# One encoder step on one core: the rotation table in buffers of its own and split anew, two scan-matrix buffers, and loads and stores in another order

## The reference, cut to what matters

```python
h = rmsnorm(x) * (1 + scale) + shift            # scale, shift, gate = c @ w_ada + b_ada
q, k, v, iq, ik, iw, za, u, zs = split(h @ w_in)   # 5712 columns
# attention: an indexer scores keys, the top 256 are kept, softmax over them, then * silu(za)
# S5: per group of 16 channels a 64-dim complex diagonal state
lam_bar = exp(lam * dt); b_bar = (lam_bar - 1) / lam * b
h_t = lam_bar * h_(t-1) + b_bar @ u_t           # scan over positions, chunks of 64
y = re(c @ h_t) + d * u;  y = gelu(y) * sigmoid(gelu(y) @ w_glu + b_glu) * silu(zs)
out = x + gate * rmsnorm(concat(attn, y) @ w_out)
```

## Time and profile before

| what | value |
|---|---|
| median of 3 runs | 2255.09 us (2254.04 to 2257.56) |
| the profiled execution | 2255.6 us, its span in the trace 2253.8 us |
| mean granted clock of TensorE | 0.972 of 2.4 GHz |
| PE busy | 2107.7 us, 94% of the span |
| DVE busy | 1293.7 us, 57% |
| ACT busy | 717.1 us, 32% |
| POOL busy | 272.8 us, 12% |
| data moved | 292.90 MB, 130 GB/s on average |

### The profile page before, as it was taken

The page is one execution under the profiler, slowest core; times in us unless marked ns, Lnnn a source line. Parts: engine busy times, 40 slices in busy tenths (PEclk is TensorE's granted clock), DMA queues, the critical chain, the costliest instruction groups (busy, mean ns, idle before and its releaser), DMA issues. The chain is left out here.

```text
span 2253.8 us, 33057 instructions
## 1 busy us (share of the span) xinstructions
PE 2107.7 (94%) x12713; PEld 1860.7 (83%) x12713; DVE 1293.7 (57%) x2587; ACT 717.1 (32%) x1408; POOL 272.8 (12%) x560
## 2 busy tenths in 40 slices
PE   5898898999999999999999999599989899999996
PEld 4578797888899999999999999477877577777764
DVE  5555645344324788888877665466865354324445
ACT  5341122111124333233333221344544333223323
POOL 0254353355410000000000000000000100000000
PEclk9999999999999999999999999699999999999998
DMA  9973466665443333333333432663441232224666
GB/s 349 335 179 77 125 138 146 161 183 175 144 122 84 97 87 95 98 88 98 94 92 98 98 80 77 193 180 118 124 109 50 79 93 73 73 82 152 174 187 190
DMA packets 380718, 292.90 MB, mean 130 GB/s; under 512 B 125273, under 2 KB 317985, under 8 KB 379273
## 3 DMA queue, kind: packets, MB, share of 16 engines
q1 hardware_dynamic: 355906, 256.96, 41.6%
q10 hardware_dynamic: 23328, 30.03, 4.0%
q0 software_dynamic: 1328, 3.80, 0.5%
HBM read 230.51 MB, written 60.20 MB: 129 GB/s over the span
## 5 line engine op out<-in xcount | busy, mean ns | idle before, releaser
L1293 PE MATMUL ps_z<-h_hi,w_hi 128*128 128x384 f32 (+2 forms) x1936 | 666.4, 344 | 0.0
L1295 PE MATMUL ps_z<-h_hi,w_lo 128*128 128x384 f32 (+2 forms) x1936 | 657.0, 339 | 0.0
L1294 PE MATMUL ps_z<-h_lo,w_hi 128*128 128x384 f32 (+2 forms) x1936 | 656.8, 339 | 0.0
L1293 PEld LDWEIGHTS ps_z<-h_hi,w_hi 128*128 128x128 f32 (+1 forms) x1936 | 363.1, 188 | 15.6 <-issue 5.2
L1294 PEld LDWEIGHTS ps_z<-h_lo,w_hi 128*128 128x128 f32 (+1 forms) x1936 | 363.2, 188 | 5.1
L1295 PEld LDWEIGHTS ps_z<-h_hi,w_lo 128*128 128x128 f32 (+1 forms) x1936 | 362.8, 187 | 5.4
L877 DVE TENSOR_TENSOR w_lo<-w_raw,w_hi 128x512 fp32r<-128x512 f32 (+1 forms) x172 | 125.5, 730 | 352.8 <-ACT w_hi L543 351.1
L543 ACT ACTIVATE w_hi<-w_raw 128x512 fp32r<-128x512 f32 (+1 forms) x172 | 107.5, 627 | 262.9 <-DMA w_raw<-in_w_in 204.5
L1009 DVE MAX8 top<-score 128x8 f32<-128x1024 f32 (+5 forms) x192 | 171.1, 891 | 3.4
L1011 DVE MATCH_REPLACE8 score<-top,score 128x1024 f32<-128x1024 f32 (+5 forms) x192 | 168.2, 876 | 0.0
L2304 POOL DMA_DIRECT2D v_cached<-in_cache_v x8 | 6.0, 753 | 1157.1 <-POOLq L66 1133.2
(11 more groups left out here) (455 smaller groups left out, 3272.8 us busy)
## 6 DMA issues: line engine op xcount, KB each, us to landing
w_raw<-in_w_in SPq DMA_DIRECT2D x176, 256.0 KB, 3.1
wada<-in_w_ada SPq DMA_DIRECT2D x32, 1024.0 KB, 9.1
o_raw<-in_w_out SPq DMA_DIRECT2D x92, 256.0 KB, 3.1
wg<-in_w_ada SPq DMA_DIRECT2D x32, 512.0 KB, 5.0
zt<-z_sb ACTq DMA_DIRECT2D x28, 576.0 KB, 4.2
ssm_f<-in_w_out SPq DMA_DIRECT2D x52, 256.0 KB, 4.2
g_raw<-in_w_glu SPq DMA_DIRECT2D x24, 512.0 KB, 4.3
xs<-in_x_prompt SPq DMA_DIRECT2D x8, 1024.0 KB, 7.9
```

The source lines that it names most:

```text
L1293: M(to, w_hi[q][:, k, 0:m], h_hi[:, kk, cols], start=kk == 0, stop=False)
L1294: M(to, w_hi[q][:, k, 0:m], h_lo[:, kk, cols], start=False, stop=False)
L1295: return M(to, w_lo[q][:, k, 0:m], h_hi[:, kk, cols], start=False, stop=kk == KB - 1)
```

## The change

The change has these parts. A block `extra` of 8 KB a partition is set aside. GpSimd's two rotation buffers move there, so they overlap nothing; GpSimd makes six turns of the rotation table and VectorE two (slots 14 and 15), and GpSimd no longer waits for `c_mat_T`. The second `turn_c` moves from slot 12 to 13. Later a second `wmat` and `bslot` lie in `extra`, and batches alternate. The clearing of `taps` follows the first `pmat`. `load_states` moves from slot 36 to 35. The store of the last block has a semaphore of its own, `z_last`, which only the load of `za` in the next program awaits; that load becomes the last of the first four. `ROW_STEP` becomes 0, 2, 3, 5, 6 and so on, `gate_tanh(0)` and `gates(0)` move one step later. In `attend_samples` the two pieces of `w_out` are loaded after the keys of samples 2 and 3. In `project_out` the half-rows of pair 0 are stored from GpSimd's queue. Some semaphores are merged or divided, and the scratch for DMA descriptors is set to 8192.

```diff
--- before.py
+++ after.py
@@ -130,6 +130,8 @@
         w_hi = [sb(f"w_hi{q}", [P, QK, P], F32R) for q in range(4)]
+        extra = (nc.sbuf_base + 31) // 32 * 32
+        sb("extra", [P, 2048])
         z_sb = sb("z_sb", [P, TOK])
@@ -156,12 +158,15 @@
         turn_w = over(back + 35328, "turn_w", [P, 3, PAIRS, 8])
-        chunk = [[over(back + at, f"rot_chunk{i}_{at}", [P, 4, 2, 8, 16]) for at in ats] for i, ats in enumerate(((20992,), (12800, 16896)))]
-        chunk_w = [over(back + at, f"rot_work{i}", [P, 4, 8, 16]) for i, at in enumerate((25088, 27136))]
-        wmat, wtmp, pmat, ptmp, bslot, pout, taps, skip = placed(
-            keep["back_free"], ("wmat", [P, PAIR_BATCH, 2, STEP + 1, CH]), ("wtmp", [P, PAIR_BATCH, STEP + 1, CH]),
-            ("pmat", [P, PAIR_BATCH, 2, STEP, CH]), ("ptmp", [P, PAIR_BATCH, STEP, CH]), ("bslot", [P, 2, PAIR_BATCH, CH]),
+        chunk = [[over(back + at, f"rot_chunk{i}_{at}", [P, 4, 2, 8, 16]) for at in ats] for i, ats in enumerate(((extra - back, extra - back + 4096), (12800, 16896)))]
+        chunk_w = [over(back + at, f"rot_work{i}", [P, 4, 8, 16]) for i, at in enumerate((35328, 27136))]
+        wmat0, wtmp, pmat, ptmp, bslot0, pout, taps, skip = placed(
+            keep["back_free"], ("wmat0", [P, PAIR_BATCH, 2, STEP + 1, CH]), ("wtmp", [P, PAIR_BATCH, STEP + 1, CH]),
+            ("pmat", [P, PAIR_BATCH, 2, STEP, CH]), ("ptmp", [P, PAIR_BATCH, STEP, CH]), ("bslot0", [P, 2, PAIR_BATCH, CH]),
             ("pout", [P, PAIR_BATCH, 2, P]), ("taps", [CH, 2 * PAIR_BATCH, TAPS, CH]), ("skip", [CH, 2 * PAIR_BATCH, CH]))
+
+        wmat = [wmat0, over(extra, "wmat1", [P, PAIR_BATCH, 2, STEP + 1, CH])]
+        bslot = [bslot0, over(extra + 8 * PAIR_BATCH * (STEP + 1) * CH, "bslot1", [P, 2, PAIR_BATCH, CH])]
 
@@ -194,7 +199,7 @@
         rows_in, s5_in, bc_in, x_in, ada_in = sem("rows_in"), sem("s5_in"), sem("bc_in"), sems("x_in", 4), sems("ada_in", 7)
-        ident_step, ident_ok, c_copied, vec_T, vec_copied = (sem(n) for n in ("ident_step", "ident_ok", "c_copied", "vec_T", "vec_copied"))
+        ident_ok, c_copied, vec_T, vec_copied = (sem(n) for n in ("ident_ok", "c_copied", "vec_T", "vec_copied"))
         squared, var_ok, root_ok, x_scaled, norm_step = (sem(n) for n in ("squared", "var_ok", "root_ok", "x_scaled", "norm_step"))
@@ -209,7 +214,7 @@
         p_step, p_ok, p_T, p_copied, p_out = (sem(n) for n in ("p_step", "p_ok", "p_T", "p_copied", "p_out"))
-        bslot_ok, w_step, w_ok, q_stored = (sem(n) for n in ("bslot_ok", "w_step", "w_ok", "q_stored"))
+        bslot_ok, w_step, w_ok, q_stored = sem("bslot_ok"), sem("w_step"), sem("w_ok"), sems("q_stored", 2)
         k_mm, k_copied, skip_ok, taps_ok, taps_zero, toep_stored = (
...
@@ -251,6 +258,7 @@
         SCAN = BUILD + 2 * BATCHES + 2
+        POOL_TURNS, DVE_TURNS = 6, 2
         HALVES = PAIRS // 2
@@ -312,7 +320,7 @@
 
-            pairs = slice(12 * i + 4 * n, 12 * i + 4 * n + 4)
+            pairs = slice(4 * (POOL_TURNS * i + n), 4 * (POOL_TURNS * i + n + 1))
             mine = chunk[i][n % len(chunk[i])]
@@ -327,8 +335,8 @@
         def store_chunk(eng, i, n):
-            pairs = slice(12 * i + 4 * n, 12 * i + 4 * n + 4)
-            eng.dma_start(scr["rot"][:, pairs], chunk[i][n % len(chunk[i])][:].rearrange("p j r a b -> p j r (a b)")).then_inc(rot_out[i + n % len(chunk[i])], 16)
+            pairs = slice(4 * (POOL_TURNS * i + n), 4 * (POOL_TURNS * i + n + 1))
+            eng.dma_start(scr["rot"][:, pairs], chunk[i][n % len(chunk[i])][:].rearrange("p j r a b -> p j r (a b)")).then_inc(rot_out[2 if i else n % 2], 16)
 
@@ -393,7 +401,7 @@
                 sp.dma_start(scr["s5_out"][:, js],
-                             wmat[:, :, :, 1:].rearrange("p j r t c -> p j r (t c)")).then_inc(q_stored, 16)
+                             wmat[b % 2][:, :, :, 1:].rearrange("p j r t c -> p j r (t c)")).then_inc(q_stored[b % 2], 16)
 
@@ -496,22 +504,24 @@
                     store_inputs(batch_at(S - 2))
-                if 16 <= S < 21:
-                    sp.wait_ge(chunk_ok[1], S - 15)
-                    store_chunk(sp, 1, S - 16)
+                if 15 <= S < 15 + DVE_TURNS:
+                    sp.wait_ge(chunk_ok[1], S - 14)
+                    store_chunk(sp, 1, S - 15)
                 if G + 1 < N:
...
                     store_taps(batch_at(S - 3))
+                if S == SCAN - 3:
+                    load_states()
                 if S == SCAN - 2:
                     load_half(0)
-                    load_states()
                 if S == SCAN:
...
                     sp.wait_ge(toep_stored, 16 * STEP * BATCHES)
-                    sp.wait_ge(q_stored, 16 * BATCHES)
+                    for i in range(2):
+                        sp.wait_ge(q_stored[i], 8 * BATCHES)
                     sp.wait_ge(p_out, 16 * BATCHES)
@@ -569,7 +579,7 @@
                 else:
-                    act.dma_start(zt[col:col + m, c0:], z_sb[0:m, c0:]).then_inc(z_out, 16)
+                    act.dma_start(zt[col:col + m, c0:], z_sb[0:m, c0:]).then_inc(z_out if G < N - 1 else z_last, 16)
 
@@ -722,14 +732,14 @@
             store(N - 1)
-            act.wait_ge(z_out, stored_before[N])
+            act.wait_ge(z_out, stored_before[N - 1])
             act.wait_ge(g_out, 16 * GATE_UNITS)
...
             G_ = nc.gpsimd
-            G_.memset(ident[:], 0.0).then_inc(ident_step, 1)
-            pool.wait_ge(ident_step, 1)
+            G_.memset(ident[:], 0.0).then_inc(ident_ok, 1)
+            pool.wait_ge(ident_ok, 1)
             G_.affine_select(out=ident[:], in_=ident[:], compare_op=ALU.not_equal, fill=1.0, base=0,
@@ -791,16 +801,13 @@
             pool.sem_inc(turn_ok, 1)
-            pool.wait_ge(c_mat_T, 2)
-            for n in range(3):
-                if n:
-                    pool.wait_ge(rot_out[0], 16 * n)
+            for n in range(POOL_TURNS):
+                if n >= 2:
+                    pool.wait_ge(rot_out[n % 2], 16 * (n // 2))
                 rotations(G_, pool, 0, n)
                 store_chunk(pool, 0, n)
-            for i in range(3):
-                pool.wait_ge(rot_out[i], (48, 48, 32)[i])
+            pool.wait_ge(rot_out[2], 16 * DVE_TURNS)
             pool.wait_ge(c_read, 2)
-            G_.memset(taps[:], 0.0).then_inc(taps_zero, 1)
 
@@ -816,11 +823,14 @@
                     pool.wait_ge(p_ok, 2 * b + ri + 1)
+                if b == 0:
+                    G_.memset(taps[:], 0.0).then_inc(taps_zero, 1)
 
...
             pool.wait_ge(p_out, 16 * BATCHES)
-            pool.wait_ge(q_stored, 16 * BATCHES)
+            for i in range(2):
+                pool.wait_ge(q_stored[i], 8 * BATCHES)
             pool.wait_ge(toep_stored, 16 * STEP * BATCHES)
@@ -891,24 +901,29 @@
                 flat = lambda t: t.rearrange("p j t c -> p j (t c)")
+                mine, s = wmat[b % 2], b % 2
                 if part_ == 0:
+                    if b >= 2:
+                        dve.wait_ge(k_mm, b - 1)
+                        dve.wait_ge(q_stored[s], 16 * (b // 2))
+                    elif b:
+                        for i in range(2):
+                            dve.wait_ge(rot_out[i], 8 * POOL_TURNS)
+                    else:
+                        dve.wait_ge(rot_out[2], 16 * DVE_TURNS)
+                    V.tensor_copy(bslot[s][:], bbar[:, :, js, :]).then_inc(bslot_ok, 1)
+                    V.tensor_tensor(mine[:, :, 0], pr, cr, ALU.mult).then_inc(w_step, 1)
                     if b:
-                        dve.wait_ge(k_mm, b)
-                    else:
-                        dve.wait_ge(taps_zero, 1)
-                    V.tensor_copy(bslot[:], bbar[:, :, js, :]).then_inc(bslot_ok, 1)
-                    if b:
-                        dve.wait_ge(q_stored, 16 * b)
-                    V.tensor_tensor(wmat[:, :, 0], pr, cr, ALU.mult).then_inc(w_step, 1)
+                        dve.wait_ge(w_ok, b)
                     V.tensor_tensor(wtmp[:], pi, ci, ALU.mult).then_inc(w_step, 1)
-                    V.tensor_tensor(wmat[:, :, 1], pi, cr, ALU.mult).then_inc(w_step, 1)
+                    V.tensor_tensor(mine[:, :, 1], pi, cr, ALU.mult).then_inc(w_step, 1)
                 else:
                     dve.wait_ge(w_step, b * 5 + 3)
-                    V.tensor_tensor(wmat[:, :, 0], wmat[:, :, 0], wtmp[:], ALU.subtract).then_inc(w_step, 1)
+                    V.tensor_tensor(mine[:, :, 0], mine[:, :, 0], wtmp[:], ALU.subtract).then_inc(w_step, 1)
                     dve.wait_ge(w_step, b * 5 + 4)
...
                     dve.wait_ge(w_step, b * 5 + 5)
-                    V.scalar_tensor_tensor(flat(wmat[:, :, 1]), flat(wmat[:, :, 1]), -1.0, flat(wtmp[:]),
+                    V.scalar_tensor_tensor(flat(mine[:, :, 1]), flat(mine[:, :, 1]), -1.0, flat(wtmp[:]),
                                            ALU.mult, ALU.subtract).then_inc(w_ok, 1)
@@ -923,7 +938,8 @@
                 if j == 0:
-                    dve.wait_ge(q_stored, 16 * BATCHES)
```

(62 more changed lines are left out.)

## The result

The changed kernel is slower: 2265.99 us in the median of 19 runs (2255.9 to 2275.0) against 2255.09 of the kernel before (2251.0 to 2261.2), ratio 1.0052, interval 1.0041 to 1.0062. The forecast was 2250 with a range of 2242 to 2259, so even its sign was wrong. The profiled execution took 2268.6 us, its span is 2266.6, 12.8 longer than before.

What follows compares the result with a forecast made beforehand. TensorE works almost all the time, so only its waits count. Terms +6.2 + 3.5 + 0 - 3.3 - 6 - 4 - 1.3 = -4.9 took 2255.6 to 2250.7; forecast 2250 us, range 2242 to 2259.

Steps and rivals of the forecast that it cites:

- Part 1: project_in, slots 12 to 22: GpSimd's rotations delay turn_c 25.0 us, less 6.2 and 12.4: +6.2 us (+2 to +12).
- Part 2: project_in, slot 20: a wait for wmat(0), hidden before behind the pmat wait, comes out: +3.5 us (0 to +5).
- Part 5: Start of gate_and_attend: earlier start, vT sooner, za off the head of the engines' order: -6 us (-2.5 to -11).
- Part 6: attend_samples: keys loaded ahead of weights save 2.8 us of wait and 1.2 of clock: -4 us (-5.8 to 0).
- Part 4: States loaded a slot earlier: shorter state_rows wait, scan inputs the next wait: -3.3 us (-5 to 0).
- Part 7: project_out: half-rows stored by GpSimd remove a TensorE wait of 1.28 us: -1.3 us (-2 to +1).
- 11 in a turn of 8.3 us: project_in: VectorE gets 11 instructions through per GpSimd turn, so 55 take 5 turns and turn_c comes at about 219 us.
- the far end: project_in: VectorE loses every change, some 33 GpSimd instructions come between, 31 us of delay, to 225 us.
- the row of 168 to 172 us: Profile before: VectorE fits 18 short instructions and GpSimd 15 into 4 us, each busy over 85%.
- Rival (b): project_in: VectorE loses each change, turn_c at 225 us or later, longer wmat(0) wait: 2259 to 2261 us; chance 0.15.
- Part 3: Two scan-matrix buffers: VectorE's wait of 5.88 us goes but no TensorE wait hangs on it: 0 (-4 to 0).
- rival (c): gate_and_attend: za is the new wait, Part 5 keeps 2.5 us: 2254 us; chance 0.15 together with another rival.

Runs made afterwards that it cites:

- e5_keys_back: The changed kernel with the two pieces of w_out loaded ahead of the keys of samples 2 and 3 again; 2265.5 us.
- Experiments 1 and 2: First: changed kernel, GpSimd's six turns held until VectorE copied C's first half, 2242.6 us. Second: kernel before, only GpSimd's three turns started early, 2268.8 us.
- experiment 4: The version of experiment 3 with seven turns on GpSimd and one on VectorE, and Part 6 undone; 2241.3 us.
- experiment 3: Changed kernel with the second turn_c in two other PSUM banks, VectorE's preparation spread over slots 9 to 16, its turns in 17 and 18; 2237.6 us.
- experiment 6: The changed kernel with a wait between the two products of each pair in GpSimd's turns; one execution, 2256.0 us.
- Experiment 8: The kernel before with Part 5 alone; 2253.5 us, ratio 0.9994.

## Why the prediction was wrong, by its own steps

The forecast sum was -4.9 us, the trace has +12.8. Of the 17.7 us between, parts 1 and 2 together make 5.2 (14.9 in place of 9.7), part 5 makes 3.3, part 6 makes 5.6, and parts 4 and 7 make 3.6. Part 1 alone is 8.8 too low, the largest miss, and part 2 takes some of that back; with part 1 at its +6.2 the sum would still have come out above zero.

**Part 1** had the mechanism and the place right and the size wrong. The failed step is "11 in a turn of 8.3 us": one VectorE instruction for each GpSimd instruction and five in each pause, so five turns and 219 us. In the changed kernel VectorE got 7 through at the 12 changes from a first to a second product, 17 at the 12 from there to a sum, 29 at the 11 behind a sum, pauses among them. That is about six a turn beside GpSimd's instructions, as I had it, but in the first five pauses only 5, 4, 4, 3 and 3: an instruction that began late in the issue of the store was held over both products of the next pair (2.55 us at 182.51, above). It makes some nine in a turn of 8.5 us, and all 36 GpSimd instructions came ahead of the end, beyond the far end of 33 that I gave. `turn_c` was 33.6 us later where I had 25.0 (31 at the far end). In the second trace of this project_in (e5_keys_back) it was 30.0 us later, with 33 GpSimd instructions ahead of the end: the step fails there too, by less.

The rest of the working holds: +33.6 - 6.2 - 12.4 = +15.0, and the first small matmuls of `wmat(0)` start 14.9 us later than before (288.79 against 273.9). (The recorded sum with 25.0 gives +6.4, not +6.2, and that of part 2 gives 3.3, not 3.5; neither matters here.) Experiments 1 and 2 show the cause from both sides. That the copies out of PSUM are free of it was right: in experiment 4 the eight of them take 3.73 us beside GpSimd's seventh turn, and 3.73 in experiment 3, where GpSimd is done. I had taken it that VectorE gets in at each change. It did at all 12 where GpSimd waits for its own result, ahead of a sum, but at only 7 of the 12 without such a wait; with a wait there (experiment 6) it did at all 12. The rule that the prediction cites from the Trainium skill ("SBUF — State Buffer", "SBUF: two separate sides"), that the loser blocks, gave the better size here; the row of 168 to 172 us still speaks against a lock for whole instructions where both are short. Rival (b) had the direction, but its 225 us and 2259 to 2261 still fell short, and the longer wait for `wmat(0)` that it counted on did not come.

**Part 2** named a wait of 3.5 us; here it is 0.69. The term mis-sized is the eight stores, 6.55 us at the like place but here

```profile
275.61 3.73 ACTq L579 DMA_DIRECT2D u<-z_sb  x8
```

with no store of SP between them, where seven stood at the like place; I had taken off 1, not 2.8. Another 0.8 us is not accounted for. No run isolates what made the stores quicker: eight of them also took 6.54 us at 223.90 in the kernel before, with one load of SP between. In experiment 4 the wait was there with 3.82 us; there the stores took 4.78 us and VectorE's building beside GpSimd 10.7, where it took 8.1 here.

**Part 3** gave nothing, as said: the `wmat` waits of 2.3, 2.3 and 6.2 us are the same.

**Part 4** has the next wait that it named, 3.09 us for the scan's inputs in place of 4.17 for the states. From the first `wmat` to the scan's matmuls of 454.85 before and 467.37 after, the shift falls from 14.9 to 12.5, -2.4 of the -3.3; a wait and a lower clock near 675 us take 1.6 of it back.

**Part 5** was right on the start (-2.2 of -2.5) and on `vT` (-2.9 of -2.0), and wrong on what follows: rival (c) holds. ScalarE, then TensorE in the changed kernel:

```profile
1441.55 1.06 ACT L1837 ACTIVATE gate<-za 128x1024 f32<-128x1024 f32 x1 [4.34 <-DMA za<-zt]
...
1444.31 0.48 PE L2151 MATMUL ps_t<-ident,probs 128*128 128x128 f32 x1 [2.64 <-DVE probs L1945]
...
1460.19 0.48 PE L2151 MATMUL ps_t<-ident,probs 128*128 128x128 f32 x1 [7.72 <-DVE probs L1945]
```

ScalarE stands 4.34 us for `za`, now the last load, then the steps behind it wait, and the wait behind the roundings of the values has grown from 5.9 to 7.7 us. gate_and_attend is 0.5 us shorter, not 3.5. Experiment 8 agrees, and so do the other traces: gate_and_attend takes 341.6 us in the mean of the nine that have this part and 341.3 in the five that don't.

**Part 6** had the wait right (under 2 us):

```profile
1777.00 0.66 PE L2394 MATMUL ps_ks<-ident,k_cached_pre 128*128 128x128 f32 x4 [1.43 <-DMA k_cached_pre<-in_cache_k]
```

but the stage took 42.33 us, not 36.7, with TensorE's granted clock low behind that wait: 0.63 in 1776 to 1786 us, 0.86 in the next 10 and 0.83 in the 20 after that (0.89 in 1762 to 1803 us, nearly the whole stage, before). In other executions with this order it took 38.0 to 40.7 (42.5 once), without it 40.2 to 42.2: 1.3 less in the mean of all traces, not 4.

**Part 7** gave 0.2 us where I had 1.3: the wait of 1.28 us is gone from the trace, but project_out took 450.0 to 452.6 us in the seven other traces that have it and 450.3 to 453.2 in those that don't, so no gain is told from the spread.

## What to carry to other kernels

Work that is moved to an idle GpSimd is not free if VectorE has many short instructions at that time on a path that TensorE waits for: count 0.8 to 0.9 us of delay for each GpSimd instruction that falls into that run (33.6 us for 36, 30.0 for 33 and 14.6 for 18 here), not only for the changes that VectorE may lose, and ask whether the idle time was there because someone was spared. The cheapest cure is the order: either GpSimd waits for the end of the critical run (one wait, -23 us here), or the critical run is taken off TensorE's path (-28 us). And price a moved wait together with what it hid: the gains of single waits here came back as the next wait a few us further on.

## What the runs showed of the hardware that I had not expected

GpSimd does not share the delay: in the changed kernel's trace most of its rotation instructions keep their 1.05 to 1.3 us (1.6 at most, beside 128x512 on VectorE), while those of VectorE's 128x32 instructions that are held up go from 0.19 to between 0.93 and 2.6 us. Two GpSimd instructions issued without a wait between them can pass as one: the second begins 0.05 us ahead of the recorded end of the first, and VectorE got an instruction in between in 7 of 12 cases, with a wait there in 12 of 12. All five cases without one are the first pair behind the issue of a store.

The time of the changed kernel varies by 19 us from run to run, that of the kernel before by 10. A part of that seems to lie in this contention: the two traces of the same project_in differ by 5.9 us from GpSimd's first rotation to the second `turn_c`, and project_in ends 6.5 us apart (1427.3 and 1420.8).
